# Down's last four steps walked pair by pair with the last norm among them, and a new order of work at the opening of the second feed-forward stage

## The chip, the cores and the metric

The kernel runs on one core of one Trainium2 chip. A core has five engines that run side by side and meet through semaphores: TensorE (PE, with its weight loads PEld), VectorE (DVE), ScalarE (ACT), GpSimd (POOL) and SyncE (SP), which here issues DMAs. The metric is device time in microseconds, the median of three runs. "Span" is the time from the first to the last instruction of one profiled execution. PE writes into eight PSUM banks of 128x512 float32. A bank can be used again once VectorE or ScalarE has emptied it.

## What is computed

One layer of a hybrid encoder over 1024 tokens of width 1024. The change touches only the two feed-forward stages, above all the second, and the norm behind it:

```
def _rms_norm(v, g):
    r = lax.rsqrt(jnp.mean(vf * vf, axis=-1, keepdims=True) + EPS)
    return (vf * r).astype(v.dtype) * g

def _swiglu(u, w_gate, w_up, w_down):
    return (jax.nn.silu(u @ w_gate) * (u @ w_up)) @ w_down

h = h + 0.5 * _swiglu(_rms_norm(h, ffn1_norm[l]), ffn1_w_gate[l], ...)
...                                # gated mixers, cross-attention
h = h + 0.5 * _swiglu(_rms_norm(h, ffn2_norm[l]), ffn2_w_gate[l], ffn2_w_up[l], ffn2_w_down[l])
return _rms_norm(h, final_norm)
```

D_FF is 2816, so w_gate and w_up are 1024x2816 and w_down is 2816x1024.

## The kernel before

**Layout and precision.** h lies transposed: eight tiles h[:, m] of 128 features by 1024 tokens. Every product is done as three matmuls of 128x128 by 128x512 with the operands split into a high and a low part (w_hi by x_hi, w_hi by x_lo, w_lo by x_hi), all through `mm` at L499.

**Gate and up.** Both matrices together are treated as 2x2 blocks and multiplied with seven products instead of eight. The stage has FT = 22 rounds n, each of seven products i (names in GU_ORDER, for round 0 in GU_FIRST). A product has KP = 4 contraction steps kp of three matmuls, so 12 matmuls, and fills one bank. Products s1, s3, w22 and s2 read xt (sums of blocks of the input), w11, w12 and s4 read xb (the input's blocks). VectorE adds the finished banks into f_g (even n, the gate) or acc and sq (odd n, up) at L1991. Two rounds, even and odd, make a pair whose activation (act_sum, L1597 and L2164) SP stores to DRAM (act_store). ScalarE may copy the first bank of the next even round (L1254) only when that store has landed, since f_g is read by it.

**Weights.** SP loads raw blocks, GpSimd forms sums of them (L1037), ScalarE writes w_hi (block_high, L1169) and GpSimd w_lo (L1018). Six slots hold them: the w_hi of a product waits until PE has finished the product six places earlier.

**Banks.** RING_USES lists the uses of the eight banks in order. A use takes the bank of the one eight places earlier, and `wait_bank` makes PE wait until that one has been emptied.

**Opening of the second stage (f = 1).** The stage starts before its norm is known: the products run on h times the gain, and the factor 1/rms comes later. `opening_raw` makes the operands, on ScalarE xt_hi, xb_hi (L1203, L1204) and squares (L1178), on VectorE xt_lo and xb_lo (`x_low`, L1921). PE runs round 0 in two parts, each kp by kp: first s1, s2, s3 and w22 on xt, then w11, w12 and s4 on xb. The sums of squares go over the partitions in 16 short PE instructions (L654) ahead of product (1,1). `factor_diag` on VectorE (L1603, L1631, L1597, L1641, with the root on ScalarE at L1109) makes diagonals of the factor, and two pairs of matmuls ahead of (1,5) spread them over two banks ("spread"). VectorE copies them to rn (L2047) and scales gate by it.

**Down.** Seven such products s with FP = 11 contraction steps kp each, 77 steps d = 11 s + kp. A step has 12 matmuls: for each of the four pairs mp of output tiles three. A step needs its activation, as xt_hi by ScalarE (`act_high`, L1362, four slots, so it waits for step d - 4) and xt_lo by VectorE (`act_low`, L2168), and its weights, w_lo here by VectorE too (`w_low`, L2178). Product 6 adds only to the first 512 tokens ("half 0") of the even tiles. So the second half of h is final after product 5, and its last norm is worked out beside product 6: squares (L1330, L1342), VectorE's adds into acc, `last_sums` on PE (L696), `factor_diag`, `last_spread` (L702, L703), `scale_last` (L2130) and the store to `out`. Half 0 follows at the very end. The numbers LAST_SUMS = 71, LAST_SPREAD = 74, LAST_FACTOR = 75 and LAST_ROOT = 71 say ahead of or behind which step d PE, VectorE and ScalarE do their part of this.

The order of each engine's work is written out by hand, one program per engine. No scheduler moves it.

## Time and profile before

| | us |
|---|---|
| median of the runs | 2174.71 (2174.01 to 2175.9) |
| the profiled execution | 2178.96 |
| its span | 2177.2 |
| mean granted TensorE clock | 0.978 |

PE is busy for 2065.0 us of the span, VectorE for 1441.3, GpSimd for 1182.5, ScalarE for 638.0. In a time line a row gives start, duration, engine, line, operation, what is written and read, the shape, how many instructions were merged, and in brackets the idle time of the engine before it and what ended it. Times are from the start of the span. Sub-shapes of two dimensions are shown as their product, and a merged row shows the shape of its first.

### The profile page before, as it was taken

To read this page: it belongs to the slowest core of one execution; us is meant where nothing else is said; L and a number is where in the kernel's file an instruction comes from. 1 tells how busy PE (TensorE), PEld (TensorE's weight loads), DVE (VectorE), ACT (ScalarE), POOL (GpSimd) and SP (SyncE) were. 2 spreads that over 40 slices of the span, in tenths; PEclk is the share of its full clock that TensorE was granted. 3 is DMA by queue.
4 is the path that set the end of the run, shared out by engine and by line. 5 is a ranking of instruction groups with operands and counts; after the bars stand their busy time and mean duration, and the time that the engine had idled before them with its cause. 6 is when DMAs were issued, how large, how long until landed. Compare 5 with 4: busy or idle time off the path is not lost.

```text
span 2177.2 us, 24452 instructions
## 1 busy us (share of the span) xinstructions
PE 2065.0 (95%) x9194; PEld 1685.2 (77%) x9194; DVE 1441.3 (66%) x1653; ACT 638.0 (29%) x978; POOL 1182.5 (54%) x752
## 2 busy tenths in 40 slices
PE   6899999999999998999998999898899999999995
PEld 5487788888878877778886888787688888887784
DVE  7767597656776978553334365546776767787686
ACT  4333223233344500001112123325222323244451
POOL 2078778877555522113333322036599999984550
PEclk9899999999999999999999999999999999999997
DMA  6333343445767461321113141211123232277762
GB/s 223 134 118 111 112 148 134 157 140 186 274 238 245 135 178 56 106 71 61 49 49 116 49 165 59 100 46 47 65 93 126 92 112 94 89 253 268 246 225 93
DMA packets 139764, 286.37 MB, mean 132 GB/s; under 512 B 12288, under 2 KB 37504, under 8 KB 139008
## 3 DMA queue, kind: packets, MB, share of 16 engines
q1 hardware_dynamic: 97424, 226.53, 29.9%
q10 hardware_dynamic: 42224, 58.29, 8.1%
q8 instruction: 74, 1.21, 0.2%
q14 instruction: 42, 0.34, 0.0%
HBM read 222.39 MB, written 63.42 MB: 131 GB/s over the span
## 4 chain that ended last, share of the span: by engine, by line
PE 67%; DVE 20%; DMA 5%; issue 3%; ACT 2%; POOL 2%; SPq 1%; DVEq 0%; ACTq 0%
PE ps L499 65%; DMA raw<-in_dn 4%; DVE w_lo L2178 3%; DVE xt_lo L2168 2%; DVE h L2187 2%; DVE f_g L1597 1%; DVE acc L1597 1%; POOL w_lo L1018 1%; POOL raw L1085 1%; DVE ua_lo L1597 1%; DVE ua_lo L1606 1%; PE ps L758 1%; ACT w_hi L1169 1%; DMA d_act<-f_g 1%; DVE tables L1597 0%
## 5 line engine op out<-in xcount | busy, mean ns | idle before, releaser
L1018 POOL TENSOR_TENSOR w_lo<-raw,w_hi 128x512 fp32r<-128x512 f32 x352 | 544.8, 1564 | 242.4 <-ACT w_hi L1169 242.2
L499 PE MATMUL ps<-xt_hi,w_hi 128*128 128x512 f32 x1320 | 519.7, 394 | 16.3 <-DVE xt_lo L2168 5.6
L499 PE MATMUL ps<-xt_hi,w_lo 128*128 128x512 f32 x1320 | 516.6, 391 | 0.0
L499 PE MATMUL ps<-xt_lo,w_hi 128*128 128x512 f32 x1320 | 516.4, 391 | 0.0
L1169 ACT ACTIVATE w_hi<-raw 128x512 fp32r<-128x512 f32 x462 | 279.0, 626 | 517.4 <-POOL raw L1037 257.6
L1026 POOL TENSOR_SCALAR w_hi<-raw 128x1024 fp32r<-128x1024 f32 x54 | 61.0, 1130 | 510.3 <-PE ps L499 502.7
L499 PEld LDWEIGHTS ps<-xt_hi,w_hi 128*128 128x128 f32 x1320 | 249.4, 189 | 77.1 <-issue 18.1
L1037 POOL TENSOR_TENSOR raw<-raw 128x512 f32<-128x512 f32 x178 | 273.6, 1547 | 49.1 <-DMA raw<-in_gu 41.9
L499 PEld LDWEIGHTS ps<-xt_hi,w_lo 128*128 128x128 f32 x1320 | 249.4, 189 | 52.7
L499 PEld LDWEIGHTS ps<-xt_lo,w_hi 128*128 128x128 f32 x1320 | 249.5, 189 | 51.2 <-issue 0.2
L499 PE MATMUL ps<-ua_hi,w_hi 128*128 128x512 f32 x608 | 241.4, 397 | 10.5 <-DVE ua_lo L1597 6.8
L1085 POOL TENSOR_TENSOR raw<-raw 128x512 f32<-128x512 f32 x110 | 164.9, 1511 | 141.1 <-DMA raw<-in_dn 141.0
L499 PE MATMUL ps<-ua_lo,w_hi 128*128 128x512 f32 x608 | 239.2, 393 | 0.0
L499 PE MATMUL ps<-xb_hi,w_hi 128*128 128x512 f32 x528 | 208.6, 395 | 9.7 <-POOL w_lo L1018 5.1
L499 PE MATMUL ps<-xb_lo,w_hi 128*128 128x512 f32 x528 | 207.1, 392 | 0.0
L499 PE MATMUL ps<-xb_hi,w_lo 128*128 128x512 f32 x528 | 207.0, 392 | 0.0
L1991 DVE TENSOR_TENSOR f_g<-ps,f_g 128x512 f32<-128x512 f32 x158 | 109.1, 691 | 122.3 <-ACT f_g L1254 109.8
L499 PE MATMUL ps<-ua_hi,w_lo 128*128 128x512 f32 x608 | 188.4, 391 | 0.0
L1028 POOL TENSOR_TENSOR w_lo<-raw,w_hi 128x1024 fp32r<-128x1024 f32 x54 | 144.9, 2684 | 4.5
L499 PEld LDWEIGHTS ps<-ua_hi,w_hi 128*128 128x128 f32 x608 | 116.0, 191 | 38.9 <-DVE ua_lo L1597 5.2
L2178 DVE TENSOR_TENSOR w_lo<-raw,w_hi 128x512 fp32r<-128x512 f32 x110 | 113.2, 1029 | 49.1 <-ACT w_hi L1169 48.2
L499 PEld LDWEIGHTS ps<-ua_lo,w_hi 128*128 128x128 f32 x608 | 116.0, 191 | 23.8
(308 smaller groups left out, 2886.7 us busy)
## 6 DMA issues: line engine op xcount, KB each, us to landing
raw<-in_dn SPq DMA_DIRECT2D x264, 256.0 KB, 3.4
raw<-in_gu SPq DMA_DIRECT2D x88, 512.0 KB, 5.5
raw<-in_weights SPq DMA_DIRECT2D x54, 512.0 KB, 3.5
d_act<-acc SPq DMA_DIRECT2D x20, 512.0 KB, 2.8
d_act<-sq SPq DMA_DIRECT2D x20, 512.0 KB, 3.8
d_act<-f_g SPq DMA_DIRECT2D x20, 512.0 KB, 4.7
raw<-in_kv SPq DMA_DIRECT2D x16, 512.0 KB, 3.5
xt_hi<-d_act SPq DMA_DIRECT2D x8, 1024.0 KB, 7.2
```

What stands on the lines that cost most here:

```text
L499: ins = nc.tensor.matmul(out, lhsT, rhs, start=start, stop=stop)
L1018: add(lo, src, hi.bitcast(F32), op=ALU.subtract).then_inc(s_w_low["pool"], 1)
L1026: nc.gpsimd.tensor_scalar(hi, src, 1.0, 0.0, ALU.mult, ALU.add).then_inc(s_w_hi, 1)
L1028: add(lo, src, hi.bitcast(F32), op=ALU.subtract).then_inc(s_w_low["pool"], 1)
L1037: add(out, x, y, op=op).then_inc(s_w_sum, 1)
L1085: add(raw_part(op, 0), raw_part(op, 0), raw_part(op, 1), op=ALU.add if w[2] > 0 else ALU.subtract).then_inc(s_w_sum, 1)
L1169: nc.scalar.activation(w_hi[:, op.halves[0]].rearrange("p k c -> p (k c)"), src, ACT.Copy).then_inc(s_w_high, 1)
L1597: link(v.tensor_tensor(out, x, y, op), tally)
L1991: link(v.tensor_tensor(out, x, y, ALU.add), adds)
L2168: v.tensor_tensor(xt_lo[:, 3, d % 4], acts_at(d // FP, d % FP), xt_hi[:, 3, d % 4].bitcast(F32), ALU.subtract).then_inc(s_a_lo, 1)
L2178: v.tensor_tensor(lo, raw_part(op, 0), hi.bitcast(F32), ALU.subtract).then_inc(s_w_low["dve"], 1)
L2187: v.scalar_tensor_tensor(out=x, in0=bank, scalar=0.5 * sign, in1=x, op0=ALU.mult, op1=ALU.add).then_inc(s_dev, 1)
```

## The change

**Opening.** In both stages PE runs the contraction steps of s4 later: s4's kp 0 and 1 come behind the kp 1 of w11 and w12. In the second stage ScalarE writes s4's w_hi between the second and the third pair of xb_hi instead of behind the squares. VectorE adds the last two squares ahead of round 0's four first adds, then does all nine adds of round 0, and only then `factor_diag`. The spread moves from ahead of product (1,5) to ahead of (1,6), and in round 1 VectorE does the four adds of `halves` ahead of the two multiplications of the silu with rn.

**Down.** In the second stage the steps d = 73 to 76 no longer run step by step with four pairs each, but pair by pair with four steps each. PE's `last_sums(1)` moves from ahead of d = 71 to ahead of pair 1, `last_spread(1)` from ahead of d = 74 to ahead of pair 3. ScalarE's root moves from behind act_high of d = 75 to behind that of d = 76, VectorE's `factor_diag` behind the last act_low. The adds of half 0's squares move between the emptyings of the four last banks, the scalings of half 1 are spread over the end, and three of them stand behind the last `factor_diag`.

```
-LAST_SUMS, LAST_SPREAD, LAST_FACTOR, LAST_ROOT = 71, 74, 75, 71
+LAST_STEPS, LAST_SUMS, LAST_SPREAD, LAST_ROOT = 4, 1, 3, 73
+SUMS_AT, SPREAD_AT = (1, 1), (1, 6)
...
-                uses += [("sums",)] if (n, i) == (1, 1) else [("spread", 0), ("spread", 1)] if (n, i) == (1, 5) else []
+                uses += [("sums",)] if (n, i) == SUMS_AT else [("spread", 0), ("spread", 1)] if (n, i) == SPREAD_AT else []
...
+                for kp in range(KP):
+                    pe.wait_ge(s_xb_lo, 2 * (KP * f + kp + 1))
+                    for op in first[4:6]:
+                        first_pass(op, kp)
+                    for k in ((), (0, 1), (2,), (3,))[kp]:
+                        first_pass(first[6], k)
...
+                apart = DN_N - LAST_STEPS if f else DN_N
+                for d in range(apart):
+                    op = next(passes)
+                    wait_low(op)
+                    pe.wait_ge(s_a_lo, DN_N * f + d + 1)
+                    for mp in range(MP):
+                        if d % FP == 0:
+                            wait_bank("dn", d // FP, mp)
+                        dn_pass(op, d, mp)
+                if f:
+                    ops = [next(passes) for _ in range(LAST_STEPS)]
+                    for mp in range(MP):
+                        if mp == LAST_SUMS:
                             last_sums(1)
+                        if mp == LAST_SPREAD:
                             last_spread(1)
+                        for op, d in zip(ops, range(apart, DN_N)):
+                            if mp == 0:
+                                wait_low(op)
+                                pe.wait_ge(s_a_lo, DN_N * f + d + 1)
+                            dn_pass(op, d, mp)
...
+                        if k == 1:
+                            block_high(ops[6])
...
-                        block_high(ops[j + 6])
+                        if f == 0 or j:
+                            block_high(ops[j + 6])
...
+                if f:
+                    add_squares(KT - 2)
+                    add_squares(KT - 1)
                 copied(0, 1)
                 op_done(0, 3)
...
-                if f:
-                    add_squares(KT - 2)
-                    add_squares(KT - 1)
-                    factor_diag(ffn_bank(f, "sums"), L, s_diag)
                 op_done(0, 6)
...
+                if f:
+                    factor_diag(ffn_bank(f, "sums"), L, s_diag)
...
                         scale(0, 1)
                         scale(0, 0)
+                        op_done(n, 5)
+                        halves(q, F)
...
                 if f == 1:
-                    for m in range(MP):
-                        scale_last(m, 1)
+                    factor_diag(last_bank(1, 0), HALF, s_fac)
                 for mp in range(MP):
                     evacuate(f, len(DN) - 1, mp)
...
+                    if f == 1 and mp:
+                        add_last(mp - 1, 0)
+                    if f == 1 and mp == 2:
+                        for m in range(3):
+                            scale_last(m, 1)
...
-                    for m in range(MP, KT):
+                    add_last(MP - 1, 0)
+                    for m in range(3, 5):
                         scale_last(m, 1)
-                    for q in range(MP):
-                        add_last(q, 0)
                     factor_diag(last_bank(0, 0), HALF, s_fac)
+                    for m in range(5, KT):
+                        scale_last(m, 1)
                     for m in range(KT):
                         scale_last(m, 0)
```

What stands in the engines' rows at three places follows. ScalarE at the opening of the second stage, before: the four pairs of xb_hi, the squares, then w_hi of s4 and of (1,0) and (1,1).

```order
L1203 ACTIVATE xb_hi<-h,gains 128x512
L1204 ACTIVATE xb_hi<-h,gains 128x2x512
L1203 ACTIVATE xb_hi<-h,gains 128x512
L1204 ACTIVATE xb_hi<-h,gains 128x2x512
L1178 ACTIVATE sq<-h 128x1024
L1178 ACTIVATE rn<-h 128x1024
L1169 ACTIVATE w_hi<-raw 128x512 x3
L1254 ACTIVATE f_g<-ps 128x512
```

The same place now:

```order
L1226 ACTIVATE xb_hi<-h,gains 128x2x512
L1191 ACTIVATE w_hi<-raw 128x512
L1225 ACTIVATE xb_hi<-h,gains 128x512
L1226 ACTIVATE xb_hi<-h,gains 128x2x512
L1225 ACTIVATE xb_hi<-h,gains 128x512
L1226 ACTIVATE xb_hi<-h,gains 128x2x512
L1200 ACTIVATE sq<-h 128x1024
L1200 ACTIVATE rn<-h 128x1024
L1191 ACTIVATE w_hi<-raw 128x512 x2
L1278 ACTIVATE f_g<-ps 128x512
```

One w_hi, that of s4, has moved ahead of four xb_hi and two squares. VectorE in rounds 0 and 1 of the second stage, before (f_g<-ps is round 0, acc and sq<-ps round 1; rows of the factor are left out):

```order
L1991 TENSOR_TENSOR f_g<-ps,f_g 128x512 x4
L1910 TENSOR_TENSOR acc<-acc,sq 128x1024
L1910 TENSOR_TENSOR acc<-acc,rn 128x1024
L1603 TENSOR_SCALAR norm<-ps 128x8
...
L1641 TENSOR_TENSOR diag_lo<-ident,norm 128x1024
L1991 TENSOR_TENSOR f_g<-ps,f_g 128x512 x5
L1991 TENSOR_TENSOR acc<-ps,acc 128x512 x2
L2047 COPY rn<-ps 128x512 x2
L2028 SCALAR_TENSOR_TENSOR f_g<-f_g,rn 128x1024
L2030 TENSOR_TENSOR f_g<-f_g,rn 128x1024
L1597 TENSOR_TENSOR f_g<-f_g,rn 128x1024 x2
L1991 TENSOR_TENSOR sq<-ps,acc 128x512
```

The same place now:

```order
L1935 TENSOR_TENSOR acc<-acc,sq 128x1024
L1935 TENSOR_TENSOR acc<-acc,rn 128x1024
L2016 TENSOR_TENSOR f_g<-ps,f_g 128x512 x9
L1628 TENSOR_SCALAR norm<-ps 128x8
...
L1666 TENSOR_TENSOR diag_lo<-ident,norm 128x1024
L2016 TENSOR_TENSOR acc<-ps,acc 128x512 x2
L2079 COPY rn<-ps 128x512 x2
L2054 SCALAR_TENSOR_TENSOR f_g<-f_g,rn 128x1024
L2056 TENSOR_TENSOR f_g<-f_g,rn 128x1024
L2016 TENSOR_TENSOR sq<-ps,acc 128x512
L2016 TENSOR_TENSOR sq<-ps,sq 128x512 x2
```

All nine adds of round 0 stand ahead of the factor, and round 1's adds into sq ahead of the silu's multiplications. VectorE at the end of Down, before (from the last w_lo on; xt_lo from prep is step 76):

```order
L2178 TENSOR_TENSOR w_lo<-raw,w_hi 128x512
L2168 TENSOR_TENSOR xt_lo<-xt_lo,xt_hi 128x512
L1603 TENSOR_SCALAR norm<-ps 128x4
...
L1641 TENSOR_TENSOR diag_lo<-ident,norm 128x512
L2168 TENSOR_TENSOR xt_lo<-prep,xt_hi 128x512
L2130 SCALAR_TENSOR_TENSOR h<-h,gains,ps 128x512 x4
L2187 SCALAR_TENSOR_TENSOR h<-ps,h 128x512
```

The same place now:

```order
L2203 TENSOR_TENSOR xt_lo<-prep,xt_hi 128x512
L1628 TENSOR_SCALAR norm<-ps 128x4
...
L1666 TENSOR_TENSOR diag_lo<-ident,norm 128x512
L2222 SCALAR_TENSOR_TENSOR h<-ps,h 128x512
L1682 MEMSET stat 128x1
L2222 SCALAR_TENSOR_TENSOR h<-ps,h 128x512
L1682 MEMSET stat 128x1
L1622 TENSOR_TENSOR acc<-acc,f_g 128x512
L2222 SCALAR_TENSOR_TENSOR h<-ps,h 128x512
L1682 MEMSET stat 128x1
L1622 TENSOR_TENSOR acc<-acc,f_g 128x512
L2167 SCALAR_TENSOR_TENSOR h<-h,gains,ps 128x512 x3
```

Step 76's xt_lo is ahead of the factor, and the adds into acc stand among the emptyings.

## Rows read from the trace of the kernel before

**Rows 1.** The page, part 1: busy time, share of span, instructions.

```profile
PE 2065.0 (95%) x9194; PEld 1685.2 (77%) x9194; DVE 1441.3 (66%) x1653; ACT 638.0 (29%) x978; POOL 1182.5 (54%) x752
```

**Rows 2.** Time line of PE: start, us, what; in brackets idle before, what ended it.

```profile
1504.42 0.76 PE L499 MATMUL ps<-xb_hi,w_hi 128*128 128x512 f32 x1 [5.13 <-POOL w_lo L1018]
...
1516.30 1.84 PE L654 MATMUL ps<-ones,acc 128*128 128x1 f32 x16
...
1532.01 0.77 PE L499 MATMUL ps<-xt_hi,w_hi 128*128 128x512 f32 x1 [5.54 <-issue]
...
1551.31 0.50 PE L499 MATMUL ps<-xt_hi,w_hi 128*128 128x512 f32 x1 [2.39 <-DVE acc L1991]
...
1568.10 0.50 PE L499 MATMUL ps<-xb_hi,w_hi 128*128 128x512 f32 x1 [0.17 <-ACT f_g L1254]
...
2134.75 1.84 PE L696 MATMUL ps<-ones,acc 128*128 128x1 f32 x8 [7.09 <-DVE acc L1597]
...
2162.60 1.84 PE L696 MATMUL ps<-ones,acc 128*128 128x1 f32 x8 [7.05 <-DVE acc L1597]
```

**Rows 3.** Stretches: us, then busy (x instructions) per engine, PEclk, DMA share, GB/s.

```profile
1505.80:1509.20 3.40, 3.40 (x9) 2.63 (x8) 3.31 (x3) 0.63 (x1) 3.32 (x3) 0.50 0.82 274
...
1550.20:1553.60 3.40, 2.29 (x10) 1.91 (x11) 3.30 (x4) 0.00 (x0) 3.32 (x3) 1.00 0.00 0
...
1610.00:1840.00 230.00, 230.00 (x1015) 189.97 (x1014) 170.19 (x153) 66.42 (x109) 216.05 (x134) 1.00 0.30 103
...
2137.30:2140.70 3.40, 3.40 (x9) 2.63 (x9) 0.00 (x0) 0.00 (x0) 0.00 (x0) 0.50 0.00 0
```

**Rows 4.** Time line of ACT, opening of the second stage and end of Down.

```profile
1496.63 0.70 ACT L1203 ACTIVATE xb_hi<-h,gains 128x512 fp32r<-128x512 f32 x1
...
1501.82 1.65 ACT L1169 ACTIVATE w_hi<-raw 128x512 fp32r<-128x512 f32 x3
...
1567.45 0.60 ACT L1254 ACTIVATE f_g<-ps 128x512 f32<-128x512 f32 x1 [12.36 <-DMA d_act<-f_g]
...
1605.76 0.60 ACT L1254 ACTIVATE f_g<-ps 128x512 f32<-128x512 f32 x1 [9.48 <-DMA d_act<-f_g]
...
2142.16 1.28 ACT L1109 ACT_TABLE_LOAD   x1
```

**Rows 5.** Time line of DVE, opening of the second stage.

```profile
1501.21 1.93 DVE L1921 SCALAR_TENSOR_TENSOR xb_lo<-h,gains,xb_hi 128x512 fp32r<-128x512 f32 x2
...
1506.89 2.29 DVE L1910 TENSOR_TENSOR acc<-acc,sq 128x1024 f32<-128x1024 f32 x1
...
1520.91 0.20 DVE L1631 RECIPROCAL norm<-norm 128x8 f32<-128x8 f32 x1 [2.50 <-ACT norm L1109]
...
1527.68 2.17 DVE L1641 TENSOR_TENSOR diag_lo<-ident,norm 128x1024 fp32r<-128x1024 f32 x1
1529.78 3.58 DVE L1991 TENSOR_TENSOR f_g<-ps,f_g 128x512 f32<-128x512 f32 x5
...
1538.13 1.29 DVE L2047 COPY rn<-ps 128x512 f32<-128x512 f32 x2 [3.32 <-PE ps L499]
...
1559.21 0.69 DVE L2164 TENSOR_TENSOR sq<-sq,acc 128x512 f32<-128x512 f32 x1
```

**Rows 6.** Time line of DVE, end of Down and the last norm.

```profile
2131.98 0.69 DVE L2168 TENSOR_TENSOR xt_lo<-xt_lo,xt_hi 128x512 fp32r<-128x512 f32 x1
...
2136.45 0.68 DVE L2178 TENSOR_TENSOR w_lo<-raw,w_hi 128x512 fp32r<-128x512 f32 x1
...
2153.55 0.69 DVE L2187 SCALAR_TENSOR_TENSOR h<-ps,h 128x512 f32<-128x512 f32 x1 [3.42 <-PE ps L499]
...
2164.55 0.16 DVE L1603 TENSOR_SCALAR norm<-ps 128x4 f32<-128x4 f32 x1 [2.09 <-PE ps L696]
...
2167.18 0.69 DVE L1641 TENSOR_TENSOR diag_lo<-ident,norm 128x512 fp32r<-128x512 f32 x1
...
2169.18 5.35 DVE L2130 SCALAR_TENSOR_TENSOR h<-h,gains,ps 128x512 f32<-128x512 f32 x8 [1.31 <-PE ps L703]
```

More of the change, by code:

```diff
@@ L656, in ffn @@
                             ins.then_inc(s_norm, 1)
-                        if f == 1 and n == 1 and i == 5:
+                        if f == 1 and (n, i) == SPREAD_AT:
                             pe.wait_ge(s_diag, 1)
@@ L668, in ffn, with dn_pass @@
                             gu_pass(op, ffn_bank(f, "gu", n, i), kp)
-                for s in range(len(DN)):
-                    for kp in range(FP):
-                        op, d = next(passes), s * FP + kp
-                        if f == 1 and d == LAST_SUMS:
+                def dn_pass(op, d, mp):
+                    s, kp = d // FP, d % FP
+                    bank = ffn_bank(f, "dn", s, mp)
+                    ahi, alo = xt_hi[:, 3, d % 4], xt_lo[:, 3, d % 4]
+                    h = op.halves[0]
+                    end = kp == FP - 1
+                    mm(bank, w_hi[:, h, mp], ahi, kp == 0, False)
+                    mm(bank, w_hi[:, h, mp], alo, False, False)
+                    mm(bank, w_lo[:, h, mp], ahi, False, end,
+                       signal=s_dbank if end else s_dstep if mp == MP - 1 else None)
@@ L2034, in scale, with halves @@
                         ins.then_inc(s_gate, 1)
+                def halves(q, F):
+                    add(F[1][:, C0], q["s3"], F[0][:, C1])
+                    add(F[1][:, C1], q["s1"], F[1][:, C0])
+                    add(F[1][:, C0], q["w22"], F[1][:, C0])
+                    add(F[0][:, C1], q["s1"], F[0][:, C1])
                 for n in range(1, FT):
@@ L2059, in ffn @@
                         act_low(f, 1)
-                    op_done(n, 5)
-                    add(F[1][:, C0], q["s3"], F[0][:, C1])
-                    add(F[1][:, C1], q["s1"], F[1][:, C0])
-                    add(F[1][:, C0], q["w22"], F[1][:, C0])
-                    add(F[0][:, C1], q["s1"], F[0][:, C1])
+                    if not (f and n == 1):
+                        op_done(n, 5)
+                        halves(q, F)
                     scale(n, 1)
```

38 lines of the change are left out of this document (10 added, 28 removed).

## The prediction

> **What bounds the kernel now.** I read the page first: PE is busy 95% of the span [rows 1], so a change that moves matmuls without removing any can only win PE's waits and the work ahead of its first and behind its last matmul. Then PE's time line, at the two places that the diff touches. Three waits stand at the opening of the second stage, 5.13, 5.54 and 2.39 us, and two in the last norm, 7.09 and 7.05 us [rows 2]. Then the stretches: the granted clock is 0.50, that is 1.2 GHz, in 1505.8 to 1509.2 and in 2137.3 to 2140.7, both behind such waits, with 9 matmuls in 3.40 us, and 1.00 (2.4 GHz) in the steady part, where 1015 matmuls take 230.0 us, 0.227 each, so 2.72 for a product of twelve. A wait of 2.39 us left it at 1.00 [rows 3]. At half clock a matmul costs some 0.2 us more, and about eleven run so behind each long wait: 2.2 us. Last I read who ends each wait, on ScalarE and VectorE [rows 4 to 6].
>
> **Opening, step by step.** (a) The 5.13 us wait is for s4's low part. ScalarE writes its high part behind eight xb_hi and two squares, from 1501.82; the change puts it where the third pair begins, 1496.63 [rows 4], and s4's first matmuls stand behind kp 1. The wait goes, with its slow clock. What is late next is VectorE's xb_lo, which ends at 1503.14 [rows 5]. GpSimd's low part of s4 and its next sum now run beside it. The row with contention is the squares' add, 2.29 us for 1024 columns, and an xb_lo pair without it takes 1.93 for 512 and 1024 together [rows 5], so I add about 1 us: 1504.4. In 1505.8 to 1509.2 both engines were busy throughout and VectorE finished three instructions [rows 3]. By that rule x_low is hit and round 0's adds are not; without it the sum would keep 1503.1 and win 1 us more.
>
> PE then runs from xb_lo's second pair, at about 1500.7, 30 matmuls without a pause (6.8 us), ends round 0 near 1507.5 and works on: six products of round 1 at 2.72 and sums at 1.84 [rows 2] bring it to the spread at 1525.6.
> (b) The 5.54 us wait is for a bank of round 0: the adds at 1529.78 stood behind the factor [rows 5]. Now all nine stand ahead of it (9 x 0.72 = 6.5 us, from about 1508.9), so that wait goes too. What is late next is the factor. ScalarE takes the root behind (1,6)'s w_hi, and this needs GpSimd's fourth sum of round 1: from 1503, where the w_hi of (1,0) is written, seven GpSimd instructions at 216.05 / 134 = 1.6 us [rows 3], then the w_hi, 0.6, and a table load, 1.28 [rows 4]: about 1516. From the reciprocal to the end of diag_lo it took 1520.91 to 1529.85, 8.9 us [rows 5], with GpSimd at work; the same again gives 1525 to 1526. Uncontended its parts would sum to about half, and PE would be last: the spread lies between 1525.6 and 1527. I take 1526.3, and the copies into rn at 1527.3, where they were at 1538.13: **10.8 us earlier**.
> (c) From those copies to the end of the activation sum VectorE worked without a gap: 1538.13 to 1559.90, 21.8 us [rows 5]. The four adds only change places in it. The store, its landing and ScalarE's copy follow: the copy ends at 1568.05 [rows 4], and PE's product (3,1) starts at 1568.10 behind it [rows 2]. So (3,1) can't start before 1557.3. PE itself, with nine products behind the spread, is there at about 1552. The 2.39 us wait for the adds of round 1 goes (they come before the silu), and a new wait of 5 us stands ahead of (3,1). Two such waits, 5.13 and 5.54, took the clock to 0.50, so I charge 2.2 us, less 0.8 that PE lost behind (3,1) anyway: 9.4 us stay. From there on PE is dense to the end of the stage, and everything that follows is timed from PE, so these 9.4 us reach the end. Bounds: 12 if the clock stays and the VectorE chain meets less contention, 6.5 if it meets more.
> (d) In the first stage s4's place changes too. PE waits for nothing there that it would win, nothing removed, nothing added: 0.
>
> **Down's end, step by step.** (e) PE waits 7.09 us ahead of d = 71, from 2127.5, for squares that VectorE adds until 2134.6, and runs some eleven matmuls at half clock [rows 2, 3]. Without that wait it is held by its operands. VectorE's order up to the last w_lo is unchanged and without gaps: step 72's xt_lo ends at 2132.67, the last w_lo at 2137.13 [rows 6]. Then come the xt_lo of 75 and 76, 0.6 each, 2138.4. PE does 71 and 72 in pieces by 2135.5, pair 0 of the last four steps by 2139.2 (its step 76 is the latest), the sums in 0.9 to 1.84, here 0.9, as sixteen took 1.84 at full clock [rows 2], then three pairs (8.2) and the spread (0.45): 2148.8. It was 2155.5.
> (f) Behind it VectorE is the bound. The factor took 3.3 us from norm to diag_lo (2164.55 to 2167.87) [rows 6]; ScalarE's table load of 1.28 [rows 4] stands behind act_high of 76 now, in free time. So the factor is done at 2143.6. Then four emptyings at 0.85 (0.69 and a memset), four adds at 0.72, three scalings at 0.67: 8.3, so 2152.0. Before, the last emptying, four scalings and four adds ended at 2162.5. Of the ends: sums 1.84, norm at 2154.1, factor done 2157.4, three left-over scalings 2.0 (they cover PE's spread, 1.3, which was waited for [rows 6]), eight scalings 5.35: 2164.8. It was 2169.18 + 5.35 = 2174.53. **9.8 us earlier.** The stores follow at the scalings' pace as before; eleven in a row instead of eight may cost 0.1. Bounds: 10.8 with warm sums at the end, 6 with the clock down in the middle.
>
> **Sum.** 9.4 + 9.8 = 19.2 us. The profiled execution takes 2178.96 (span 2177.2 and 1.8 around it), 4.25 above the median, and would go to 2159.8; the median goes from 2174.71 to 2155.5.
>
> **Rivals.**
> *The clock stays up ahead of (3,1).* The wait may be cut in two or shortened by 1 to 2 us, and 2.39 us left the clock alone [rows 3]. Then 11 instead of 9.4 at the opening: 2153.9. Against it: 5 us is as long as the waits that did take it down.
> *The clock falls in the pieces of Down's end.* From 2127.5 to 2139 PE works in pieces with waits of up to 1.5 us. If the clock halves there, the waits hide it up to pair 0, but the sums (1.84 instead of 0.9) and eleven matmuls behind them (2.2) come on top: 3 us less, 2158.5. The Trainium skill says it in TensorE: Matmul & The Clock Gate, "A second HAM failure mode": short idles between groups of matmuls can make the clock swing. By that rule this rival holds; the stretch 1550.2 to 1553.6, at 1.00 with 2.39 us idle around it [rows 3], speaks against it.
> *The opening only moves its wait.* If the activation store lands no earlier, (3,1) stays at 1568.1 and only Down's end is won: 2164.9. It would need a VectorE chain that isn't timed from the spread; the gapless 21.8 us speak against it.
> *The store's loop becomes the bound, and the kernel slower.* At each even round ScalarE waits for the store, with 9.48 us idle at 1605.76 too, and its copy then ended at 1606.36 [rows 4], while PE needed it about 38.1 us (14 products) behind 1568.10, at 1606.2 to 1607.2: less than 1 us of slack, nine more times. If the new phase of ScalarE, GpSimd and VectorE lengthens that loop, PE pays at every pair. It eats the 19.2 us from 2.1 + 1 us of lengthening, and from 3.6 us on (2.6 x 9 = 23.4) the kernel is slower by more than 0.2%: 2179. Against it: PE re-times the loop at every product, and GpSimd is at 216.05 of 230.00 already now [rows 3].
> *The change does nothing there*: another semaphore, hidden behind those named, holds PE at the same places: 2174.7.
>
> **How the numbers follow.** Forecast 0.68; clock up 0.10; clock down at the end 0.09; opening moved only 0.06; slower 0.04; nothing 0.03. The first three lie between 2153.9 and 2158.5; with the bounds of the unknown sizes (opening 6.5 to 12, end 6 to 10.8) the range is 2151 to 2161.5. A measurement of this kernel tells 0.2%, about 4.3 us, from no change. Faster by more: 0.93; within: 0.03; slower: 0.04.
>
> **What would show it.** PE's waits of 5.13, 5.54 and 2.39 us are gone, one of about 5 us stands ahead of (3,1), ended by ScalarE's copy, with clock 0.50 behind it; copies into rn about 10.8 us earlier; no wait for the sums ahead of pair 1, clock 1.00 through Down's end; PE's last product 6.7 us earlier relative to the first step of Down, the last scaling 9.8. Wrong I am if the spread waits for the factor by more than 1.5 us, if xb_lo ends after 1506, if even rounds from the fourth on show waits for the store, or if sums and factor of half 1 push the emptyings beyond PE's last pair.

## The result, and the profile after

| | before | after |
|---|---|---|
| median of five runs each, us | 2175.53 | 2161.11 (2157.64 to 2166.85) |
| ratio after to before, 95% interval | | 0.9942 (0.9923 to 0.9961) |
| the profiled execution, us | 2178.96 | 2157.64 |
| its span, us | 2177.2 | 2155.8 |

The change wins 0.58%, 12.6 us with an interval of 8.5 to 16.8. The forecast was 19.2 us, 2155.5, and its range ended at 2161.5. It started from 2174.71, the median of the kernel before as it was known then, and 0.9942 of that is 2162.1. Two repetitions of the changed kernel gave 0.994 (0.992 to 0.9961) and 0.9931 (0.9905 to 0.9958). So the direction was right and a third of the gain is missing.

The page, part 1, of after, to stand beside [rows 1]. PE is busy 7.8 us less, though it issues the same matmuls. Most of that isn't the change's: 4.4 us of it lie ahead of event A below, where the granted clock was 0.50 for 54.6 us before and for 44.4 after.

```profile
PE 2057.2 (95%) x9194; PEld 1679.7 (78%) x9194; DVE 1439.8 (67%) x1653; ACT 637.0 (30%) x978; POOL 1183.0 (55%) x752
```

The spans differ by 21.4 us, more than the medians, and 3.45 us of that lie ahead of the second part of the second stage's round 0. So I cut each profile at the same seven events, which all kernels of this study have: A, PE's first matmul on xb in the second stage; B, the copies into rn; C and D, ScalarE's copies behind the first and the second activation store (rounds 2 and 4); E and F, its xt_hi of Down's steps 8 and 74, the latter written when PE ends step 70; G, the end of the span. All times in us.

| kernel | A at | A to B | B to C | C to D | A to D | D to E | E to F | F to G |
|---|---|---|---|---|---|---|---|---|
| before | 1497.6 | 40.5 | 29.3 | 38.4 | 108.2 | 338.6 | 185.4 | 47.3 |
| after | 1494.2 | 35.4 | 28.3 | 40.3 | 104.0 | 339.1 | 181.6 | 37.0 |
| after, second profile | 1491.4 | 35.4 | 27.8 | 40.2 | 103.4 | 339.0 | 183.9 | 36.7 |
| after, third profile | 1489.8 | 35.4 | 28.3 | 40.5 | 104.2 | 339.2 | 181.9 | 37.3 |

The opening (A to D) won 4.2 us of a forecast 9.4, Down's end (F to G) 10.3 of 9.8. Two later kernels have the old opening ("Down's end alone" and "step by step, later" below) and took 107.2 and 107.0 us from A to D. Against 103.4 to 104.2 of the changed kernel the opening's gain is then nearer to 3.6 us. The three profiles of the changed kernel agree within 0.8 us in the stretches from A to E and from F to G, but differ by 4.4 us in when A comes and by 2.3 us in Down's middle, where nothing was changed. Much of the scatter of whole times can come from there.

**The opening after.** PE, time line as in [rows 2]; the waits of 5.13 and 5.54 us are gone. Of the four that stand there up to the sums, the first, 0.91 us, had its like before (0.89); three are new:

```profile
1494.18 0.50 PE L502 MATMUL ps<-xb_hi,w_hi 128*128 128x512 f32 x1 [0.91 <-DVE xb_lo L1946]
1498.09 0.50 PE L502 MATMUL ps<-xb_hi,w_hi 128*128 128x512 f32 x1 [2.24 <-DVE xb_lo L1946]
1503.88 0.50 PE L502 MATMUL ps<-xb_hi,w_hi 128*128 128x512 f32 x1 [0.74 <-DVE xb_lo L1946]
...
1511.24 0.94 PE L664 MATMUL ps<-ones,acc 128*128 128x1 f32 x7 [2.26 <-DVE f_g L2016]
...
1528.38 0.39 PE L502 MATMUL ps<-diag_hi,ones_r 128*128 128x512 f32 x1
...
1558.57 0.79 PE L502 MATMUL ps<-xb_hi,w_hi 128*128 128x512 f32 x1 [4.61 <-ACT f_g L1278]
```

The spread runs without a wait. The 2.26 us ahead of the sums are the wait that the forecast didn't have. The last row is (3,1), with the wait that the forecast had. In both repetitions the third of these waits was missing, the one ahead of the sums was 1.7 us, and A to B was the same 35.4. VectorE and GpSimd in the same stretch, to set beside [rows 5]:

```profile
1490.61 13.22 DVE L1946 SCALAR_TENSOR_TENSOR xb_lo<-h,gains,xb_hi 128x512 fp32r<-128x512 f32 x8 [0.43 <-ACT xb_hi L1225]
1503.75 2.30 DVE L1935 TENSOR_TENSOR acc<-acc,sq 128x1024 f32<-128x1024 f32 x1
1506.09 2.20 DVE L1935 TENSOR_TENSOR acc<-acc,rn 128x1024 f32<-128x1024 f32 x1
1508.32 6.49 DVE L2016 TENSOR_TENSOR f_g<-ps,f_g 128x512 f32<-128x512 f32 x9
...
1515.96 0.20 DVE L1656 RECIPROCAL norm<-norm 128x8 f32<-128x8 f32 x1 [0.95 <-ACT norm L1131]
...
1519.29 2.20 DVE L1666 TENSOR_TENSOR diag_lo<-ident,norm 128x1024 fp32r<-128x1024 f32 x1
...
1529.57 1.29 DVE L2079 COPY rn<-ps 128x512 f32<-128x512 f32 x2 [6.75 <-PE ps L502]
```

```profile
1489.51 3.53 POOL L1040 TENSOR_TENSOR w_lo<-raw,w_hi 128x512 fp32r<-128x512 f32 x2 [4.78 <-ACT w_hi L1191]
1493.86 1.41 POOL L1040 TENSOR_TENSOR w_lo<-raw,w_hi 128x512 fp32r<-128x512 f32 x1 [0.82 <-ACT w_hi L1191]
1495.23 1.72 POOL L1059 TENSOR_TENSOR raw<-raw 128x512 f32<-128x512 f32 x1
1499.65 1.39 POOL L1040 TENSOR_TENSOR w_lo<-raw,w_hi 128x512 fp32r<-128x512 f32 x1 [2.71 <-ACT w_hi L1191]
1501.12 1.62 POOL L1059 TENSOR_TENSOR raw<-raw 128x512 f32<-128x512 f32 x1
```

The eight xb_lo take 13.2 us. Before they took 9.1, with GpSimd idle from 1496.5 to 1502.5. GpSimd was busy during 3.1 us of those 9.1, and is during 9.7 of the 13.2. Four of the eight instructions take 1.0 us longer each than before (0.74 became 1.77, 1.27 became 2.3), the other four take the same.

**The clock.** Stretches as in [rows 3]: half clock behind the sums and behind (3,1), full clock in Down's end up to the last sums. The second row is from the second profile of the changed kernel: in both repetitions the clock also fell behind the second wait for xb_lo, which cost nothing in A to B, since VectorE held PE there.

```profile
1513.30:1516.70 3.40, 3.40 (x9) 2.67 (x9) 2.32 (x6) 2.53 (x4) 3.40 (x3) 0.50 0.00 0
```

```profile
1496.30:1499.70 3.40, 3.40 (x9) 2.64 (x8) 3.40 (x3) 1.41 (x3) 2.77 (x2) 0.51 0.19 75
```

```profile
1557.70:1561.10 3.40, 2.54 (x6) 2.05 (x7) 2.38 (x4) 2.15 (x4) 1.99 (x2) 0.50 0.62 240
...
2120.40:2123.80 3.40, 2.61 (x13) 1.84 (x12) 3.30 (x6) 0.63 (x1) 0.00 (x0) 1.00 0.00 0
2123.80:2127.20 3.40, 2.97 (x12) 1.90 (x11) 3.40 (x6) 1.92 (x2) 0.00 (x0) 1.00 0.00 0
2127.20:2130.60 3.40, 3.40 (x20) 2.94 (x20) 0.97 (x6) 0.20 (x1) 0.00 (x0) 1.00 0.02 5
```

**Down's end after.** PE, then VectorE, beside [rows 2, 6]. The 7.09 us wait has become pieces of 0.79, 0.16 and 0.27, the 7.05 us wait 2.91:

```profile
2121.87 0.47 PE L502 MATMUL ps<-xt_hi,w_hi 128*128 128x512 f32 x1 [0.79 <-DVE xt_lo L2203]
...
2128.39 0.95 PE L718 MATMUL ps<-ones,acc 128*128 128x1 f32 x8
...
2141.01 1.50 PE L718 MATMUL ps<-ones,acc 128*128 128x1 f32 x8 [2.91 <-DVE acc L1622]
```

```profile
2136.62 2.06 DVE L2167 SCALAR_TENSOR_TENSOR h<-h,gains,ps 128x512 f32<-128x512 f32 x3
2138.60 0.69 DVE L2222 SCALAR_TENSOR_TENSOR h<-ps,h 128x512 f32<-128x512 f32 x1
...
2140.18 0.69 DVE L1622 TENSOR_TENSOR acc<-acc,sq 128x512 f32<-128x512 f32 x1
...
2145.81 7.32 DVE L2167 SCALAR_TENSOR_TENSOR h<-h,gains,ps 128x512 f32<-128x512 f32 x11
```

### The profile page after: what moved, and what is told of

Its sections match the earlier page's. It is cut to its first block, busy times and chain, and to the rows that moved or that the text cites. A ratio compares the mean times of both kernels' runs of the same rounds, so it can differ in the third digit from the quotient of the medians.

```text
span 2155.8 us, 24452 instructions
## 1 busy us (share of the span) xinstructions
PE 2057.2 (95%) x9194; PEld 1679.7 (78%) x9194; DVE 1439.8 (67%) x1653; ACT 637.0 (30%) x978; POOL 1183.0 (55%) x752
## 4 chain that ended last, share of the span: by engine, by line
PE 67%; DVE 21%; DMA 5%; issue 3%; ACT 2%; POOL 1%; SPq 1%; DVEq 0%; ACTq 0%
PE ps L502 66%; DMA raw<-in_dn 3%; DVE w_lo L2213 3%; DVE xt_lo L2203 2%; DVE h L2222 2%; DVE f_g L1622 1%; DMA d_act<-f_g 1%; DVE acc L1622 1%; DVE ua_lo L1622 1%; POOL raw L1107 1%; DVE ua_lo L1631 1%; DVE xb_lo L1946 1%; DMA d_kv_lo<-xt_lo 0%; DVE sq L2016 0%; DVE tables L1622 0%
## 5 line engine op out<-in xcount | busy, mean ns | idle before, releaser
L2213 DVE TENSOR_TENSOR w_lo<-raw,w_hi 128x512 fp32r<-128x512 f32 x110 | 107.8, 980 | 42.4 <-ACT w_hi L1191 41.9
```

Source lines behind the costliest of these rows:

```text
L2213: v.tensor_tensor(lo, raw_part(op, 0), hi.bitcast(F32), ALU.subtract).then_inc(s_w_low["dve"], 1)
```

## The experiments

Each kernel was timed beside the kernel before in the same comparison. Differences between variants of different comparisons are read from the stretches, since the ratios carry the chance of each comparison. Except for the first two and "step by step, later", all are variants of the changed kernel. The stretches of all of them (A to G as above) and the ratios:

| kernel | ratio (95%) | A to B | B to C | C to D | A to D | E to F | F to G |
|---|---|---|---|---|---|---|---|
| opening alone | 0.9979 (0.9962 to 0.9996) | 37.0 | 27.6 | 40.3 | 104.8 | 180.8 | 48.1 |
| Down's end alone | 0.9962 (0.9949 to 0.9976) | 40.8 | 28.7 | 37.7 | 107.2 | 185.8 | 37.3 |
| s4 as before | 0.9937 (0.9917 to 0.9956) | 36.0 | 28.4 | 39.4 | 103.8 | 183.4 | 36.0 |
| sums later | 0.9926 (0.9901 to 0.9951) | 33.5 | 28.4 | 40.4 | 102.3 | 183.3 | 37.0 |
| spread at (1,5) | 0.9932 (0.9912 to 0.9952) | 32.7 | 28.9 | 38.8 | 100.4 | 185.5 | 36.7 |
| spread at (1,4) | 0.9924 (0.9906 to 0.9943) | 31.6 | 30.7 | 37.6 | 99.9 | 181.6 | 36.7 |
| step by step, later | 0.9985 (0.9972 to 0.9998) | 40.6 | 28.6 | 37.8 | 107.0 | 181.8 | 41.8 |
| silu earlier | 0.9909 (0.9887 to 0.9931) | 31.5 | 28.6 | 37.6 | 97.7 | 183.2 | 37.3 |
| four adds first | 0.9911 (0.9884 to 0.9938) | 34.3 | 28.3 | 39.1 | 101.7 | 187.0 | 36.7 |
| the same again | 0.993 (0.9907 to 0.9953) | 34.3 | 28.4 | 37.6 | 100.3 | 185.1 | 37.3 |
| table earlier | 0.9916 (0.9894 to 0.9938) | 33.3 | 28.4 | 40.3 | 102.1 | 180.2 | 37.1 |
| silu earlier, tail | 0.9907 (0.9882 to 0.9933) | 31.5 | 29.2 | 37.7 | 98.4 | 184.5 | 36.9 |
| all together | 0.9914 (0.989 to 0.9937) | 31.0 | 28.8 | 37.7 | 97.5 | 184.0 | 36.9 |

D to E, where none of these edits reaches, lay between 337.8 and 340.4 us. "The same again" is "four adds first" a second time, and its A to D differs by 1.4 us: a single profile doesn't settle a difference of that size. Whether s4's new place matters in the first stage can be read from the same traces. From PE's first matmul on xb there to ScalarE's copy behind the first activation store, the three profiles with the old order took 47.0 to 47.6 us, the three of the changed kernel 47.4 to 48.0.

**Each half alone.** The kernel before, with the edits of one half and the numbers and lines of the other left as they were.

> The kernel before with the opening's edits alone. Theory (read from the two profiles): the opening gained about 6 us, since in the trace of after the last step of Down that both share ends 9.6 us earlier, of which 3.45 us were there before the changed code; 2169 us where the kernel before takes 2175. Rival (the prediction's split): 9.4 us, 2165.5. Rival (the parts help each other): less than 4 us alone. In the profile: xb_lo in 13 us instead of 9, a wait of about 2.4 us ahead of the sums, one of about 5 us ahead of (3,1).

> The kernel before with the edits of Down's end alone. Theory (from the two profiles): from the last common step to the end of the span 49.7 us became 37.9, so 11.8 us, 2163 us where the kernel before takes 2175. Rival (the prediction): 9.8 us, 2165. PE's 7.09 us wait gone, clock 1.00 through the pieces, the second wait about 3 us.

Measured: 4.6 us (0.9 to 8.3) and 8.3 us (5.2 to 11.1), together 12.9, as the whole change has. Within these intervals the halves add. Down's end has its forecast size (9.8) within the interval, the opening has half of its own (9.4), which lies outside. In the opening alone the wait ahead of the sums was 1.71 us and that ahead of (3,1) 3.79.

**s4 as before.** The changed kernel with this taken back:

```
-                    for op in first[4:6]:
-                        first_pass(op, kp)
-                    for k in ((), (0, 1), (2,), (3,))[kp]:
-                        first_pass(first[6], k)
+                    for op in first[4:]:
+                        first_pass(op, kp)
...
-                        if k == 1:
-                            block_high(ops[6])
...
```

> The changed kernel with s4 of the first round as before: its w_hi behind the squares, its contraction steps not delayed. Theory (contention gives the gain back): with s4's w_lo and the next sum on GpSimd away from it, the eight xb_lo take 9 us again instead of 13.2; PE waits 5 us for s4's low part but no longer for xb_lo (2.4 and 0.9) nor ahead of the sums (2.4), since VectorE is through by then. PE reaches the sums 0 to 2 us later than in the changed kernel, and the time is within 2 us of it, 2161 to 2163. Rival (the prediction's step a): the early w_hi is worth the wait and the slow matmuls behind it, 5.1 + 2.2 less 1 us of contention, so 6 us: 2167.

The ratio is that of the changed kernel, and so is A to D. PE waits for s4's low part again, 6.26 us, with half clock behind it, and yet the opening takes no longer, since the eight xb_lo take 9.1 us again:

```profile
1500.23 0.77 PE L502 MATMUL ps<-xb_hi,w_hi 128*128 128x512 f32 x1 [6.26 <-POOL w_lo L1038]
```

```profile
1488.73 9.09 DVE L1941 SCALAR_TENSOR_TENSOR xb_lo<-h,gains,xb_hi 128x512 fp32r<-128x512 f32 x8 [0.43 <-ACT xb_hi L1223]
```

PE begins the last matmul of (1,0) 4.8 us later after A than in the first profile of the changed kernel, but finds the sums' operands ready, begins the sums only 2.3 us later and has no half clock behind them; B is 0.6 us later. The early s4, on which the forecast's step (a) rested, is worth nothing that this profile shows in this order of work.

**The wait ahead of the sums.** First the sums one product later and the four first adds ahead of the squares' adds; then that order of VectorE alone, twice; then, with the later sums, the table load ahead of the wait.

```
-SUMS_AT, SPREAD_AT = (1, 1), (1, 6)
+SUMS_AT, SPREAD_AT = (1, 2), (1, 6)
...
-                if f:
-                    add_squares(KT - 2)
-                    add_squares(KT - 1)
                 copied(0, 1)
...
                 add(F[0][:, C1], q["s1"], F[0][:, C1])
+                if f:
+                    add_squares(KT - 2)
+                    add_squares(KT - 1)
                 op_done(0, 6)
```

> The changed kernel with the sums one product later, ahead of (1,2), and round 0's four first adds ahead of the last two squares' adds. Theory (sums wait is a real loss): PE works on (1,1) in the 2.4 us that it waited, the wait and the half clock behind it go, spread and copies into rn come 4 us earlier, the wait ahead of (3,1) stays at 5 us: 4 us less than the changed kernel, 2157. Rival 1 (factor chain is the bound): the norm starts no earlier, the spread waits for the factor by the same time: 2161. Rival 2 (the store's chain is the bound and PE has slack): the wait ahead of (3,1) grows by what PE gains: 2161, with copies into rn where they were.

The wait and the half clock behind it are gone, but B comes only 1.9 us earlier, not 4; the median of 2156.51 met the expected 2157, but not by the way expected. The factor is late now: where it took 5.5 us from reciprocal to diag_lo in the changed kernel, it takes 9.6 here, and PE waits 1.41 us for it.

```profile
1516.04 0.20 DVE L1656 RECIPROCAL norm<-norm 128x8 f32<-128x8 f32 x1 [2.50 <-ACT norm L1131]
1516.27 2.03 DVE L1622 TENSOR_TENSOR norm<-norm 128x8 f32<-128x8 f32 x2
...
1518.55 1.13 DVE L1622 TENSOR_TENSOR norm<-norm 128x8 f32<-128x8 f32 x1
1519.71 1.23 DVE L1634 CAST norm_hi<-norm 128x8 fp32r<-128x8 f32 x1
1520.98 1.21 DVE L1622 TENSOR_TENSOR norm<-norm,norm_hi 128x8 f32<-128x8 f32 x1
```

Steps over eight columns that take 0.17 us alone take 1.1 to 1.2 us beside GpSimd. It was busy during 3.9 us of the 5.5, and during 9.4 of the 9.6.

> The changed kernel with round 0's four first adds ahead of the last two squares' adds, and the sums where they are. Theory (the sums wait for both, for the bank that the four adds free and for the squares): the order of the two changes nothing, the wait ahead of the sums stays at 2 to 2.5 us, now ended by the squares' add, time as the changed kernel (ratio 0.994). Rival (only the bank was in the way): the wait is 0 to 0.5 us and 2 to 4 us are won, as with the sums one product later.

> The changed kernel with round 0's four first adds ahead of the last two squares' adds, again. Theory (formed from its first trace: the four adds read a PSUM bank and take 0.69 us whether GpSimd works or not, so in the stretch in which the first square's add took 2.30 us they stand better; six instructions take 6.3 instead of 7.4 us and the wait ahead of the sums is 0.8 instead of 1.9 to 2.4 us): 1 to 3 us less than the changed kernel beside it, by whether the clock falls. Rival (its 0.9911 was the comparison's): the same as the changed kernel.

Both theories of the first run missed, the rival by little in size: the wait was 0.67 us. The order matters, but not through the bank alone. VectorE in its trace, and one row of GpSimd:

```profile
1494.85 13.17 DVE L1946 SCALAR_TENSOR_TENSOR xb_lo<-h,gains,xb_hi 128x512 fp32r<-128x512 f32 x8 [0.43 <-ACT xb_hi L1225]
1507.94 2.85 DVE L2016 TENSOR_TENSOR f_g<-ps,f_g 128x512 f32<-128x512 f32 x4
1510.83 1.23 DVE L1935 TENSOR_TENSOR acc<-acc,sq 128x1024 f32<-128x1024 f32 x1
1512.09 2.19 DVE L1935 TENSOR_TENSOR acc<-acc,rn 128x1024 f32<-128x1024 f32 x1
```

```profile
1510.91 2.29 POOL L1040 TENSOR_TENSOR w_lo<-raw,w_hi 128x512 fp32r<-128x512 f32 x1 [0.48 <-ACT w_hi L1191]
```

The same six instructions end 6.3 us behind xb_lo instead of 7.4, since the first squares' add takes 1.23 instead of 2.30 us. GpSimd was not away: its w_lo began 0.08 us behind that add and took 2.29 us, where it takes 1.3 alone. In the changed kernel a w_lo had begun 1 us ahead of the add, and the add was the longer one. The second trace shows the same pair, 1.22 and 2.31 us. The wait ahead of the sums is 0.67 us, now ended by the squares. A to B is 34.3 us in both runs, against 35.4 in all three profiles of the changed kernel, so 1.1 us are shown there; to D it is 101.7 and 100.3 against 103.4 to 104.2. The times don't show it: beside the changed kernel in one comparison it is 0.993 to 0.9931. In the two profiled executions of that comparison Down's middle took 185.1 and 181.9 us, so chance of that size can hide it.

```
+        s_table = sem("sqrt_table")
...
+                                    nc.scalar.activation(norm[:, 1, 0:1], ones[:, 0:1], ACT.Sqrt).then_inc(s_table, 1)
                                     act.wait_ge(s_norm, 5)
...
+                            act.wait_ge(s_table, 1)
                             root()
```

> The kernel with the later sums (ahead of (1,2), four adds first), and besides one element's square root on ScalarE ahead of its wait for the sums, so that the table load of 1.28 us is over when the norm comes. Theory (the factor is the bound there, PE waited 1.57 us for diag_lo): the root comes 1.3 us earlier, the wait ahead of the spread is 0.3 us, 1.3 us less than with the later sums alone, 2155 to 2157. Rival (VectorE's chain is what contention with GpSimd makes it): the chain's small steps take as much longer as they start earlier, no gain.

The root was ready 1.08 us behind the norm instead of 2.50, but from reciprocal to diag_lo it took 10.9 us instead of 9.6, and A to B stayed at 33.3. The rival holds: the chain takes what contention makes it, and starting earlier put it beside more of GpSimd's work, 10.6 us of the 10.9.

**The chain to (3,1).** The spread one and two products earlier (SPREAD_AT alone is changed), then with ScalarE's silu at i == 4 instead of 6 and `halves` behind the multiplications, as in the kernel before.

> The changed kernel with the spread ahead of (1,5), where the kernel before has it. Theory (the chain from the copies into rn over the store to (3,1) sets the opening): the factor is done at 1521.5 in the trace of after and PE would be there at 1525.7, so the copies come 2.7 us earlier, the wait ahead of (3,1) shrinks from 4.8 to about 2.1 us, and its half clock may go too: 2.7 to 4 us less than the changed kernel, 2157 to 2158.5. Rival (the factor is late in most executions, contended as in the kernel with the later sums, where it took 9.6 instead of 5.5 us): the spread waits for it, copies less than 1 us earlier, 2161.

> The changed kernel with the spread ahead of (1,4). Theory: PE is there at 1522.9 and the factor at 1521.5 where it isn't contended: copies 5.4 us earlier, the wait ahead of (3,1) gone with its half clock, 4.8 + 1.3 us less: 2155. Where the factor is contended PE waits up to 2.5 us for it, and the copies still come 2 to 3 us earlier: 2158. Rival (the chain behind the copies is held by other things, the adds of round 1 that need (1,5), and ScalarE's silu behind (1,5)): the same as with the spread at (1,5).

> The kernel with the spread ahead of (1,4), and besides ScalarE's silu of the first gate two products earlier, behind the w_hi written in product (1,3), and VectorE's four adds of halves behind the two multiplications again. Theory (the chain from the copies to the store is what holds (3,1)): with the spread at (1,4) VectorE stood idle 1.7 us ahead of the adds and multiplied from 1533.4, so the store comes 2 us earlier and the last 1.66 us of wait ahead of (3,1) go: 1 to 2 us less than with the spread at (1,4) alone, 2153 to 2157. Rival (PE is the bound now, and what it gains at (3,1) it pays elsewhere, as in waits for banks of round 1 whose adds come later): no change.

(1,5) did nearly what was expected: B 2.7 us earlier, the wait 2.51 us, but with half clock behind it. At (1,4) B comes 3.8 us earlier, not 5.4, and a wait of 1.50 us is left ahead of (3,1), with the clock at 1.00; C is 2.4 us farther behind it, since the adds of `halves` need (1,5) and stood ahead of the multiplications. With the silu earlier that is given back, and (3,1) runs without a wait and without half clock: A to D is 97.7 us, 6.2 less than in the changed kernel (103.9 on the mean of its three profiles). In the same profile D to E took 340.4 us, 1.3 more than there; with the tail's edit added it was 338.8. The row of (3,1) with the spread at (1,5), the stretch of (3,1) with all together, and ScalarE's copy there, which no longer holds anyone:

```profile
1554.47 0.50 PE L502 MATMUL ps<-xb_hi,w_hi 128*128 128x512 f32 x1 [2.51 <-ACT f_g L1278]
```

```profile
1560.00:1563.40 3.40, 3.40 (x17) 2.81 (x16) 3.26 (x5) 1.25 (x3) 3.03 (x3) 1.00 0.47 180
```

```profile
1559.10 0.60 ACT L1278 ACTIVATE f_g<-ps 128x512 f32<-128x512 f32 x1 [11.81 <-DMA d_act<-f_g]
```

**Down's end.** Is the walk pair by pair needed, or only the later places? This run keeps the old order of VectorE too. And do three scalings ahead of the last emptying hold it up?

```
-LAST_SUMS, LAST_SPREAD, LAST_FACTOR, LAST_ROOT = 71, 74, 75, 71
+LAST_SUMS, LAST_SPREAD, LAST_FACTOR, LAST_ROOT = 73, 76, 76, 73
```

> The kernel before, with step by step order kept in Down's end, and only the places changed: sums ahead of d = 73, spread ahead of d = 76, factor behind the last xt_lo. Theory (the walk pair by pair is needed since it spaces the four emptyings): PE's 7.09 us wait goes and its last product comes as early as in the kernel with Down's edits alone, but the four banks are all finished in the last step, so emptyings, adds and sums of half 0 end 3.5 to 5 us later than there: 2169 to 2171, where Down's edits alone give 2165.9. Rival (taking the wait off PE is all that counts): 2166.

The numbers are those of the theory: from F to PE's last product 18.3 us, where the changed kernel takes 19.3, but from F to G 41.8 us instead of 37.3, and 0.9985. The four emptyings start at 2146.09 and the sums wait nearly 9 us. But 2.72 us of that are four scalings that stand between the emptyings and the adds in the old order. So this run shows that the later places alone win 5.5 of some 10 us from F to G, and not how much of the rest is due to the walk pair by pair and how much to VectorE's new order. The new places with VectorE's new order and without the walk were not run. The rows, VectorE and then PE:

```profile
2146.09 0.69 DVE L2187 SCALAR_TENSOR_TENSOR h<-ps,h 128x512 f32<-128x512 f32 x1
...
2149.49 2.72 DVE L2130 SCALAR_TENSOR_TENSOR h<-h,gains,ps 128x512 f32<-128x512 f32 x4
...
2154.30 0.69 DVE L1597 TENSOR_TENSOR acc<-acc,sq 128x512 f32<-128x512 f32 x1
```

```profile
2155.14 0.56 PE L696 MATMUL ps<-ones,acc 128*128 128x1 f32 x2 [8.98 <-DVE acc L1597]
```

> The kernel with the early silu, and besides at Down's end two instead of three scalings of half 1 ahead of the last emptying, and three instead of two behind the last add. Theory (three scalings keep the last emptying 0.66 us behind PE's last product): from PE's last product to the end of the span 17.4 instead of 18.0 us, everything else as with the early silu; a time of 0.6 us less, too little for the measurement, so the trace decides. Rival (the third scaling delays the norm instead): no change.

From PE's last product to the end 17.6 us, against 18.0 with the silu earlier; but the unchanged end measured 17.4 to 18.0 in its other profiles. Not shown.

**The changed kernel again, and all together.**

> The changed kernel again, unchanged, for a second profile and more times beside the other three: the same median as before, 2161 +- 2 us. Theory (the 17.9 us by which the profile of after was shorter from round 0's second part on hold 3.8 us of chance in Down's middle, waits for xt_lo near d = 20 to 30): from the first xb product to the copy behind the store 103 to 105 us, and from d = 70 to the end 37 us, as in the first profile, but Down's middle between 181 and 186 us. Rival: all of these stretches vary alike.

> The changed kernel unchanged, to stand beside the two next ones in the same comparison, since the ratios of different comparisons differ by their rows of the kernel before. Ratio 0.994 as twice before, if the differences seen between the variants are real; 0.991 if the last comparison's rows of the kernel before were 3 us high for all.

> All that showed a gain in a trace, together: four adds first, spread ahead of (1,4), ScalarE's silu two products earlier, two scalings ahead of the last emptying. Theory (the gains add up: about 1 to 2 us from the sums' wait, 4 us from the wait ahead of (3,1), 0.4 at the end): 5 to 7 us less than the changed kernel beside it, a ratio of 0.991. Rival (at (3,1) the parts share one wait, and PE's order is now the bound): the same as four adds first alone.

The changed kernel held to its stretches and to its ratio; the median of the second comparison, 2157.7, lay 1.3 us below the range expected. All together takes 97.5 us from A to D, 6.7 less than the third profile of the changed kernel beside it, as expected; by the ratios, 0.9914 and 0.9931, it is 3.7 us, by the medians, 2157.64 and 2159.16, 1.5, and the intervals overlap. So the gain is shown from A to D and not in the whole time. It has 0.67 us of wait ahead of the sums, 1.79 for the factor ahead of the spread, and none at (3,1). The kernels with the silu earlier have ratios of 0.9907 to 0.9914. That doesn't make them the fastest: in the comparison of the first two, four adds first had 0.9911 as well, and 0.993 in the next.

## Why the prediction was right and wrong

The forecast failed in the opening, between A and the copies into rn. It had 29.7 us for that stretch (1527.3 less 1497.63), and 35.4 were measured. Of the missing 5.7 us, 2.0 are xb_lo, which (a) sized too small; 2.3 are the wait ahead of the sums and 1.7 the half clock behind it, which (b) put at nothing. Together they are 6.0, and 0.3 came back in small differences. (This is the first profile; in the repetitions the waits and slow matmuls fall otherwise, with the same 35.4.) One of the forecast's own signs of being wrong came true: xb_lo was not to end after 1506, and 9.7 us behind A is 1507.3 on the clock of the trace before.

**(a) s4's wait goes: right. What xb_lo then costs: mis-sized.** I took 1 us for GpSimd beside VectorE. I had read the trace in which GpSimd was idle for six of the nine microseconds, and the change filled them. From A to the end of xb_lo it was 5.5 us; 6.8 was forecast and 9.7 measured: 4.1 us of contention, four instructions at 1.0 us each. Round 0 ended 11.9 us behind A, not 9.9. The rule cited from SBUF — State Buffer, "Who interferes with whom", of the Trainium skill fits this trace, and its size was in my rows: an add in which both operands lay in SBUF took 2.29 us [rows 5], nearly twice the 1.22 that xt_lo of the same length took at 1491.19 with GpSimd idle. I charged it for one or two of eight instructions, not for all that GpSimd's moved work would cover.

**(b) The wait for a bank in round 0: gone there, and moved to a place that I had not looked at.** The sums take the bank of s1, eight uses earlier, and need round 0's four first adds. The change put the two squares' adds, 4.5 us of contended work, ahead of these. I checked the nine adds against the spread's banks but not against the sums'. 2.26 us of wait and 1.7 us of half clock behind it, nine matmuls at 0.43 instead of 0.23 us, are missing from the sum. The factor, which I took to be last, was done 7 us ahead of PE. It was done 27.3 us behind A, where 27.4 to 28.4 were forecast, and that was luck: the root began 3 us later than I had it, and the chain took 5.5 us, not 8.9. That made no difference here, but with the later sums it took 9.6, so neither number is a property of the code; both are of what GpSimd does then. B came 5.1 us earlier after A, not 10.8.

**(c) The chain from the copies to (3,1): right.** From the copies to the end of the activation sum 20.8 us (21.8 forecast), a wait ahead of (3,1) of 4.61 us (5), ended by ScalarE's copy, and half clock behind it; C to D is 40.3 us against 38.4, so 1.9 us, where I charged 2.2 less 0.8 (37.7 and 37.8 in the two other profiles with the old opening, so 2.6). The experiments with the spread show that this chain sets the opening. Step (d), the first stage, put at 0: right within 1 us, by the stretches given above (47.0 to 47.6 and 47.4 to 48.0 us).

**(e) Down's end: right.** The 7.09 us wait gone, clock at 1.00, F to PE's last product 6.4 us shorter (6.7 forecast). **(f)** F to G 10.3 us shorter (9.8). The last sums ran partly at half clock, as assumed.

**The rivals.** The clock stayed up in Down's pieces, so that rival fell, and with it, for waits of 0.16 to 0.79 us between the pieces, the rule that I had cited from TensorE: Matmul & The Clock Gate of the Trainium skill; both repetitions show 1.00 there too. The store's loop did not become the bound: D to E is 338.6 us before and 339.0 to 339.2 after. The opening did win, but less than half; no rival had contention give a gain back, which is what took place. The range's lower bound for the opening, 6.5 us, assumed "more contention" only in the chain behind the copies.

**The profiled execution.** I carried its difference of 4.25 us to the median as a constant, which changed nothing in 2155.5. It was chance: the profiled execution of the changed kernel lay 3.5 us below its median, and A alone moves from 1489.8 to 1500.1 among the profiles here.

## What to carry to other kernels

When a change lets one engine start earlier, price the work beside which it now runs: here an early w_hi saved a 5 us wait of PE and cost 4 us of VectorE, and by one profile won nothing. For each instruction that a change moves ahead of others, list all the waits that need the others, banks of a ring included, not only the one that the change is after. Put operations that read PSUM where the other engine reads SBUF, and measure small changes by stretches between fixed events of the trace: they repeated within 0.8 us in three profiles of the changed kernel, and within 1.5 us in two of another, where whole times moved by 10. Take two profiles of each where it matters.

## What the runs showed of the hardware

**Contention is selective, and who begins first doesn't pay.** Beside GpSimd, a VectorE add with two SBUF operands over 1024 columns took 2.2 to 2.3 us instead of 1.2, and steps over eight columns 1.1 to 1.2 instead of 0.17. An add that reads a PSUM bank took 0.69 us in either case. GpSimd was busy beside the eight xb_lo for 6.6 us more than before, and that cost VectorE 4.1.

The price hangs on what GpSimd does at the moment at which the VectorE instruction begins. From 8 us ahead of A to 60 us behind it the 17 profiles have 518 two-operand instructions of VectorE (adds, products and fused ones) with both operands in SBUF. Of these 230 began while no GpSimd instruction was under way, and all took their shortest time, though in 63 cases GpSimd began one meanwhile. The other 288 began beside one that was under way: 217 took 0.8 to 1.2 us longer, over 8, 512 or 1024 columns alike, 57 took longer by less, 14 took no longer. The 272 adds of the same stretches that read a PSUM bank all took 0.67 to 0.69 us.

**The length of a wait doesn't tell what the clock does.** I had set 2.39 us, which left it up, against 5.13, which took it down. A wait of 2.24 us for xb_lo left it at 1.00 in the first profile of the changed kernel; 2.26 us at the same place with the later sums was followed by 0.53; 1.71 us ahead of the sums, with the silu earlier, by 0.50; 1.79 us ahead of the spread, with all together, by 1.00. The wait for xb_lo stands with 2.23 to 2.26 us in 13 profiles; 11 show half clock behind it, 2 do not. A wait of 0.67 to 0.69 us ahead of the sums was followed by half clock in all three profiles that have it. The rows of the first four, in this order, first the waits of the second and third, then the stretches of the first, second and third:

```profile
1497.40 0.51 PE L502 MATMUL ps<-xb_hi,w_hi 128*128 128x512 f32 x1 [2.26 <-DVE xb_lo L1946]
```

```profile
1514.01 0.38 PE L664 MATMUL ps<-ones,acc 128*128 128x1 f32 x2 [1.71 <-DVE f_g L2016]
```

```profile
1498.90:1502.30 3.40, 3.40 (x17) 2.81 (x15) 3.40 (x3) 1.61 (x4) 2.57 (x2) 1.00 0.26 104
```

```profile
1498.30:1501.70 3.40, 3.40 (x10) 2.70 (x9) 3.40 (x3) 1.51 (x3) 2.66 (x2) 0.53 0.21 84
```

```profile
1516.80:1520.20 3.40, 3.40 (x9) 2.64 (x8) 1.89 (x6) 2.22 (x4) 2.96 (x3) 0.50 0.06 13
```

What decides it stays open; a forecast should carry about 2 us of half clock (nine to eleven matmuls at 0.2 us more) behind any such wait as a chance, not as a fact.

**Down's middle varies.** Between steps 8 and 74, which no edit touched, PE took 180.2 to 187.0 us, by waits for xt_lo: eight of them, 4.9 us in all, in the first kernel with the four adds first, one of 0.4 us in the first profile of the changed one. What makes VectorE late there in some executions was not looked into.

```profile
PE ps L502 <- DVE xt_lo L2203: 4.9, 8, 1.6
```

```profile
PE ps L502 <- DVE xt_lo L2203: 0.4, 1, 0.4
```
